# A streaming-encoder step on one core: gathers split in two passes, the last unit and the tail reordered, one decay step one unit later

## What is computed

```python
log_a = log_sigmoid(da @ w_decay + b_decay) / 16          # decays, 4 heads
...
wts = softmax(top_v) * p_g; eid = g_sel * 4 + top_i        # top-1 of 4 groups, top-2 of its 4 experts
y[token] += wts * ((silu(x @ w_gate[e]) * (x @ w_up[e])) @ w_down[e])
x = x + y
y_prompt, y_sample = rms_norm(x, norm_final)
```

## Time and profile before

| | us |
|---|---|
| median of 3 runs | 1055.69 |
| lowest, highest | 1054.32, 1058.29 |
| profiled execution | 1055.09 |
| its span | 1053.3 |
| busy TensorE, VectorE, ScalarE, POOL | 1011.3, 666.0, 539.7, 162.5 |
| granted TensorE clock, mean | 0.989 |

### The profile page before, as it was taken

The page is one execution under the profiler, slowest core; times in us unless marked ns, Lnnn a source line. Parts: engine busy times, 40 slices in busy tenths (PEclk is TensorE's granted clock), DMA queues, the critical chain, the costliest instruction groups (busy, mean ns, idle before and its releaser), DMA issues.

```text
span 1053.3 us, 16974 instructions
## 1 busy us (share of the span) xinstructions
PE 1011.3 (96%) x6950; PEld 899.4 (85%) x6950; DVE 666.0 (63%) x1009; ACT 539.7 (51%) x719; POOL 162.5 (15%) x178
## 2 busy tenths in 40 slices
PE   6999999999999999999999999999999999999984
PEld 4999899998999888888988998787788888888863
DVE  5334753453223366767665666466888989898976
ACT  5236533432223335455575633233588888878853
POOL 2111100000000123332321010031201010101061
PEclk9999999999999999999999999999999999999988
DMA  7877865527355475575363280527999999999765
GB/s 184 201 215 176 164 140 65 96 45 114 58 66 111 106 122 64 81 69 64 101 221 121 70 275 27 214 101 299 413 412 413 413 415 412 415 412 415 315 128 150
DMA packets 126172, 207.55 MB, mean 197 GB/s; under 512 B 11230, under 2 KB 68574, under 8 KB 126099
## 3 DMA queue, kind: packets, MB, share of 16 engines
q1 hardware_dynamic: 110290, 149.38, 52.4%
q0 software_dynamic: 13168, 47.59, 13.2%
q10 hardware_dynamic: 2640, 9.57, 2.3%
HBM read 174.40 MB, written 32.12 MB: 196 GB/s over the span
## 4 chain that ended last, share of the span: by engine, by line
PE 82%; DVE 5%; DMA 5%; ACT 4%; issue 3%; POOL 1%; DVEq 0%; POOLq 0%; ACTq 0%
PE ps L1222 22%; PE ps L1224 22%; PE ps L1223 22%; PE ps L1198 5%; DMA x<-y_rows,rows_i 2%; PE ps L1380 2%; PE ps L1394 2%; DMA x_rows<-h,slot_i 1%; PE ps L1356 1%; ACT w_hi L835 1%; PE ps L1340 1%; PE ps L1495 1%; PE ps L1355 1%; PE ps L1292 1%; DMA xg<-x_rows 1%
## 5 line engine op out<-in xcount | busy, mean ns | idle before, releaser
L1935 DVE TENSOR_TENSOR e_lo<-raw,e_hi 128x2048 fp32r<-128x2048 f32 x96 | 219.3, 2288 | 28.5 <-ACT e_hi L1015 28.4
L1015 ACT ACTIVATE e_hi<-raw 128x2048 fp32r<-128x2048 f32 x96 | 184.0, 1918 | 54.9 <-PE ps L1224 43.9
L1222 PE MATMUL ps<-h_hi,w_hi 128*128 128x272 f32 x632 | 186.7, 295 | 0.0
L1224 PE MATMUL ps<-h_hi,w_lo 128*128 128x272 f32 x632 | 182.3, 288 | 0.0
L1223 PE MATMUL ps<-h_lo,w_hi 128*128 128x272 f32 x632 | 181.9, 288 | 0.0
L1721 DVE TENSOR_TENSOR w_lo<-ring,w_hi 128x2048 fp32r<-128x2048 f32 (+1 forms) x40 | 72.5, 1812 | 80.1 <-ACT w_hi L835 80.1
L835 ACT ACTIVATE w_hi<-ring 128x1024 fp32r<-128x1024 f32 (+1 forms) x56 | 79.6, 1421 | 80.1 <-PE ps L1224 72.6
L1222 PEld LDWEIGHTS ps<-h_hi,w_hi 128*128 128x128 f32 x632 | 119.1, 188 | 1.2 <-issue 0.7
L1223 PEld LDWEIGHTS ps<-h_lo,w_hi 128*128 128x128 f32 x632 | 119.1, 188 | 0.2
L1224 PEld LDWEIGHTS ps<-h_hi,w_lo 128*128 128x128 f32 x632 | 118.8, 188 | 0.0
L1222 PE MATMUL ps<-w_hi,h_hi 128*128 128x256 f32 x384 | 110.0, 287 | 2.6 <-DVE va L2006 2.6
(11 more groups left out here) (432 smaller groups left out, 2040.4 us busy)
## 6 DMA issues: line engine op xcount, KB each, us to landing
raw<-in_w_gate_dram SPq DMA_DIRECT2D x32, 1024.0 KB, 10.8
raw<-in_w_up_dram SPq DMA_DIRECT2D x32, 1024.0 KB, 9.6
raw<-in_w_down_dram SPq DMA_DIRECT2D x32, 1024.0 KB, 9.8
ring<-in_w_in_dram SPq DMA_DIRECT2D x24, 1024.0 KB, 10.6
x_rows<-zero POOLq DMA_DIRECT2D x16, 512.0 KB, 7.6
ring<-in_w_in_dram SPq DMA_DIRECT2D x16, 512.0 KB, 8.4
xg<-x_rows POOLq DMA_DIRECT2D x15, 512.0 KB, 6.2
y_rows<-yo ACTq DMA_DIRECT2D x14, 512.0 KB, 6.5
```

The source lines that it names most:

```text
L1015: act.activation(e_hi[buf][:], raw[slot][:], ACT.Copy).then_inc(s_ehi, 1)
L1222: pe.matmul(out, left[0], right[0], start=first, stop=False)
L1224: return pe.matmul(out, left[1], right[0], start=False, stop=final)
L1935: dve.tensor_tensor(e_lo[slot][:], raw[slot][:], e_hi[buf][:].bitcast(F32), ALU.subtract).then_inc(s_elo, 1)
```

## The change

Seven edits:
1. `dec` 4 is behind va[9] (and behind `dec_apply` 2 there) instead of behind va[8], on all engines.
2. Unit 0: the turned rows of expert 1 come after expert 0's last up part on TensorE; ScalarE and VectorE split one more weight part before them. The row index is made after the gated product and `slot_weights_out`; the overflow counts in unit 1; the one-hots of experts 14 and 15 in units 1 and 2, one each.
3. Row 0 of `y_rows` is the zero row; expert e is stored from row 128 e + 1. The index is made of a lower and a higher slot of each token: the lower one if it is in experts 0 to 12, the other in the second column.
4. POOL: five first gathers (`y_rows[0:EARLY+1]`) once expert 12 is stored, without waiting for one another; then the slot weight of expert 15; after the store of expert 13 the five second ones.
5. Last unit: silu and gated product ahead of one weight part and more, one-hot transposes between expert 15's two down parts.
6. Tail: VectorE adds tile i, then scales tile i-1; ScalarE's square and root follow each add. `overflow` and all the rest for a full expert stand inside the branch, which comes last; in it the outputs would be made and stored a second time.
7. SyncE stores ahead of the branch.

```diff
         for f in range(GH + 2):
-            if f <= GH:
+            if f < GH:
                 hook(units_of["va"][2 * f], "dec", f)
             if f >= 2:
                 hook(units_of["va"][2 * f + 1], "dec_apply", f - 2)
+            if f == GH:
+                hook(units_of["va"][2 * f + 1], "dec", f)
...
@@ sync
+            for i in range(NTILE):
+                store(i, 0)
             with sp.If(n_ovf > 0):
+                sp.wait_ge(s_out[0], 48)
+                sp.wait_ge(s_out[1], 32)
+                sp.wait_ge(s_ovi, 3)
...
@@ gpsimd
             slot_weight(NE - 2)
-            slot_weight(NE - 1)
             pool.wait_ge(s_ovi, 1)
             pool.wait_ge(s_yst[0], 16 * LAST // 2)
+            pool.wait_ge(s_yst[1], 16 * (LAST // 2 - 1))
+            for i in range(NTILE):
+                add_rows(i, 0, rows_i, s_rows[i], y_rows[0:EARLY + 1])
+            slot_weight(NE - 1)
             pool.wait_ge(s_yst[1], 16 * LAST // 2)
-            add_rows(0, 0, rows_i, s_rows[0])
             for i in range(NTILE):
-                if i + 1 < NTILE:
-                    add_rows(i + 1, 0, rows_i, s_rows[i + 1])
                 pool.wait_ge(s_rows[i], 48)
                 add_rows(i, 1, rows_i, s_rows[i])
...
@@ scalar
             part_hi(third_after(0, 1))
+            part_hi(third_after(0, 2))
             x_out(1, 1)
-            for j in range(2, 4):
-                part_hi(third_after(0, j))
+            part_hi(third_after(0, 3))
...
             h_out(r - 1)
-            for j in range(1, 4):
+            for j in range(1, 3):
                 part_hi(third_after(r, j, 1))
             silu(r, part_of(r, 3, 1))
-            part_hi(third_after(r, 4, 1))
+            part_hi(third_after(r, 3, 1))
             act.wait_ge(s_at, NE)
             act.activation(hl_hi[:].rearrange("p c t -> p (c t)"), ps[:, 2], ACT.Copy).then_inc(s_hhi, 1)
+            part_hi(third_after(r, 4, 1))
...
+            act.activation(stat[:, 60:61], eps[:], ACT.Sqrt)
+            for i in range(NTILE):
+                act.wait_ge(s_add, i + 1)
+                squares(i)
             act.wait_ge(s_ovi, 2)
...
@@ tensor
             GU(part_of(0, 2), 0, 2, 6)
+            GU(part_of(0, 3), 0, 3, 6)
             XT(1, 1, 16)
-            GU(part_of(0, 3), 0, 3, 6)
...
             Dn(part_of(r, 5, 1), 5)
-            pe.wait_ge(s_into, 4)
+            pe.wait_ge(s_hlo, NE)
+            last_down(part_of(NE, 4), 4)
+            pe.wait_ge(s_into, 5)
             transposes(P, [(ps[:, (3, 0)[k], P * i:P * i + P], hot[:, k, i]) for k in range(2) for i in range(NTILE - 1)], s_hot)
             transposes(TS, [(ps[:, 1, TS * k:TS * k + TS], hot[0:TS, k, NTILE - 1]) for k in range(2)], s_hot)
-            pe.wait_ge(s_hlo, NE)
-            last_down(part_of(NE, 4), 4)
             last_down(part_of(NE, 5), 5)
...
@@ vector
                 step(dve.tensor_tensor(y_slot, home, ranks, ALU.add))
-                step(dve.tensor_tensor(y_slot, y_slot, away, ALU.add))
-                dve.tensor_scalar(rows_i[:], y_slot, float(LATE), None, ALU.min).then_inc(s_ovi, 1)
+                step(dve.scalar_tensor_tensor(y_slot, y_slot, 1.0, away, ALU.add, ALU.add))
+                low, high = home[:, 0:NTILE], home[:, NTILE:2 * NTILE]
+                step(dve.tensor_tensor(low, y_slot[:, 0:NTILE], y_slot[:, NTILE:2 * NTILE], ALU.min))
...
                 part_lo(third_after(r, 1, odd))
                 if not last:
                     x_out(r + 1, 1 - odd)
+                if isinstance(r, int) and r == 1:
+                    overflow_counts()
                 part_lo(third_after(r, 2, odd))
+                if isinstance(r, int) and r in (1, 2):
+                    last_one_hots(r - 1)
...
             part_lo(third_after(0, 1))
-            rows_index()
-            overflow_counts()
+            part_lo(third_after(0, 2))
             x_out(1, 1)
             gated(0, 0, 6)
             slot_weights_out()
-            for j in range(2, 4):
-                part_lo(third_after(0, j))
+            rows_index()
+            part_lo(third_after(0, 3))
...
-            part_lo(third_after(r, 1, 1))
-            last_one_hots()
-            for j in range(2, 4):
+            for j in range(1, 3):
                 part_lo(third_after(r, j, 1))
             gated(r, 1)
-            part_lo(third_after(r, 4, 1))
+            part_lo(third_after(r, 3, 1))
...
+            add(0)
+            for i in range(1, NTILE):
+                add(i)
+                finish(i - 1, 0)
+            finish(NTILE - 1, 0)
             n_ovf = dve.value_load(ovi[0:1, 0:1], min_val=0, max_val=NOVF)
             with dve.If(n_ovf > 0):
+                dve.wait_ge(s_out[0], 48)
+                dve.wait_ge(s_out[1], 32)
+                overflow()
                 late_rows()
```

More of the change, by code:

```diff
@@ L41 @@
 LATE = LAST * CAP
+EARLY = LATE - CAP
 PARTS, PART, PBUF, RAW = 6, KC * FE // 2, 3, 12
@@ L601, in _ @@
                             load_part(e, j, seq % RAW)
[L602 to L605, removed]
+                for i in range(NTILE):
+                    store(i, 1)
+                sp.wait_ge(s_out[0], 96)
+                sp.wait_ge(s_out[1], 64)
             sp.wait_ge(s_out[0], 48)
@@ L646, in _ @@
             pool.dma_start(S_in[:], state_gla[0, 0].rearrange("h k v -> k h v")).then_inc(s_sin, 16)
-            zero_blocks([(x_rows, ROWS * e) for e in range(NE)] + [(y_rows, LATE + CAP * i) for i in range(NOVF)])
-            pool.dma_start(y_rows[LATE + CAP * NOVF:].rearrange("o (a n) -> (o a) n", n=512), zero[0:2]).then_inc(s_zero, 16)
+            zero_blocks([(x_rows, ROWS * e) for e in range(NE)] + [(y_rows, LATE + 1 + CAP * i) for i in range(NOVF)])
+            pool.dma_start(y_rows[0:1].rearrange("o (a n) -> (o a) n", n=512), zero[0:2]).then_inc(s_zero, 16)
             pool.wait_ge(s_ke_mm, NTILE)
@@ L761, in slot_weight, with add_rows @@
                 pool.tensor_copy(sw_now[:, e % 2:e % 2 + 1], sw[:, e:e + 1]).then_inc(s_swn, 1)
-            def add_rows(i, k, index, done):
+            def add_rows(i, k, index, done, rows=y_rows):
                 n, col = TILES[i][1], k * NTILE + i
-                pool.indirect_dma_start(x2[0:n, i], None, y_rows, bass.IndirectOffsetOnAxis(index[0:n, col:col + 1], 0),
+                pool.indirect_dma_start(x2[0:n, i], None, rows, bass.IndirectOffsetOnAxis(index[0:n, col:col + 1], 0),
                                         compute_op=ALU.add).then_inc(done, 16)
@@ L1101, in y_out @@
                 act.wait_ge(s_y, e + 2 if isinstance(e, int) and e >= NE else e + 1)
-                row = LATE + 1 + (e - NE) * CAP if isinstance(e, int) and e >= NE else e * CAP
+                row = LATE + 1 + (e - NE) * CAP if isinstance(e, int) and e >= NE else e * CAP + 1
                 act.dma_start(y_rows[bass.ds(row, CAP)], yo[:, slot]).then_inc(s_yst[slot], 16)
@@ L1168, in _, with squares @@
             y_kept(NE - 1, 1, 1)
+            def squares(i):
+                n = TILES[i][1]
+                step(act.activation(sqf[0:n], x2[0:n, i], ACT.Square, accum_out=stat[0:n, 50 + i:51 + i]))
+                act.activation(stat[0:n, 55 + i:56 + i], stat[0:n, 50 + i:51 + i], ACT.Sqrt, bias=eps[0:n], scale=1.0 / D).then_inc(s_fsq, 1)
+            act.activation(stat[:, 60:61], eps[:], ACT.Sqrt)
+            for i in range(NTILE):
+                act.wait_ge(s_add, i + 1)
+                squares(i)
             act.wait_ge(s_ovi, 2)
@@ L1186, in _ @@
                 act.wait_ge(s_late, 16 * 2 * NTILE)
[L1187 to L1191, removed]
+                act.wait_ge(s_fo, NTILE)
+                for i in range(NTILE):
+                    squares(i)
         @block.tensor
@@ new lines, in rows_index @@
+                low, high = home[:, 0:NTILE], home[:, NTILE:2 * NTILE]
+                step(dve.tensor_tensor(low, y_slot[:, 0:NTILE], y_slot[:, NTILE:2 * NTILE], ALU.min))
+                step(dve.tensor_tensor(high, y_slot[:, 0:NTILE], y_slot[:, NTILE:2 * NTILE], ALU.max))
+                step(dve.tensor_scalar(away[:, 0:NTILE], low, float(EARLY), float(4 * NE * CAP), ALU.is_le, ALU.mult))
+                step(dve.tensor_tensor(away[:, 0:NTILE], low, away[:, 0:NTILE], ALU.add))
+                step(dve.tensor_tensor(high, high, away[:, 0:NTILE], ALU.min))
@@ new lines, in rows_index, with last_one_hots @@
+                step(dve.scalar_tensor_tensor(rows_i[:, 0:NTILE], low, float(EARLY), low, ALU.is_le, ALU.mult))
+                dve.scalar_tensor_tensor(rows_i[:, NTILE:], high, float(LATE), high, ALU.is_le, ALU.mult).then_inc(s_ovi, 1)
+            def last_one_hots(k):
+                if k == 0:
+                    dve.wait_ge(s_sc[0], 96)
+                    two = [ybase[:, 2 + q].rearrange("p (e i) -> p e i", e=2) for q in range(2)]
+                    dve.wait_ge(s_ovi, 1)
+                    step(dve.tensor_tensor(ybase[:, 1, 0:NTILE], slot_f[:, 0], slot_f[:, 1], ALU.subtract))
```

(6 more changed lines are left out.)

66 lines of the change are left out of this document (30 added, 36 removed).

## The result

| | before | after |
|---|---|---|
| median, us (8 runs each, side by side) | 1055.82 | 1050.68 |
| lowest, highest | 1054.32, 1058.63 | 1049.11, 1052.67 |
| profiled execution, its span | 1055.09, 1053.3 | 1052.25, 1050.5 |

The ratio of after to before is 0.9943, 95% interval 0.9926 to 0.9960: 5.1 us less by the medians, 6.0 by the ratio, 0.5 to 0.6%. The forecast was 1048.1 with 7.6 us of gain. The direction and the range held; by the medians, a third of the forecast gain did not come.

A forecast was written before the change was run, and what follows sets the result against it. TensorE carries 82% of the chain, so time is lost in its waits and at the end. Terms +3.9 - 0.9 - 11.0 + 0.4 = -7.6 took 1055.09 to 1047.5, with the median's 0.6 1048.1; range 1043.5 to 1052.5 us.

The forecast's parts named there:

- Part 1: Last head's decays, one unit later: ScalarE's eviction comes late and TensorE stalls, then runs at low clock; +3.9 us.
- clock term: Behind the stall for the last head's decays: 13 matmuls at granted clock 0.50; +1.25 us, between 0 and 1.3.
- Rival A: Last head's decays: the move costs nothing, as ScalarE's wait ends earlier than queued; 1044.2 us, chance 0.12.
- Part 2: Units 0 to 2 of the experts: 2.6 us gained, 1.7 lost again; net -0.9 us, bounds 0 to -2.6.
- xg wait: Unit 0: TensorE's 2.5 us wait for expert 1's rows is filled by the third up part; gain 2.6 us.
- new wait for hh: Start of unit 2: TensorE waits for the gated product, which VectorE's added small work holds; 1.7 us lost.
- the next weight part is ready ... net -0.9: Units 0 to 2: step-by-step walk of VectorE's queue, from a part ready at 753.2 to the net of -0.9 us.
- Part 3: Last unit and tail: last row 7.6 us sooner, adds and scalings interleaved, value load off the path; -11.0 us in all.
- Rival B: Tail: gathered rows stay last to come, delayed beside weights and expert 13's store; gain 5.5, not 11.0; 1053.6 us, chance 0.14.
- Rival C: Tail gathers run one at a time, the last landing at 1067; some 22 us over before, chance 0.03.
- Rival D: Unit 14: GpSimd's descriptor writing for gathers holds VectorE; +10 us, 1058, chance 0.02.
- The end: After last scaling: VectorE's value load and branch beside the last store, +0.4 us; SyncE's branch, 0 to +0.9, taken as 0.

The follow-up runs named there:

- e1: New kernel with the last head's decays back on their old unit: 1045.98 us, ratio 0.9891 to the kernel before.
- e10: New kernel with the last head's decays back on their old unit and the branch taken early on SyncE and VectorE only: 1043.28 us, ratio 0.9876 to before.
- e11: On top of e10, four small slot steps of the one-hot work on GpSimd in unit 1, both comparisons on VectorE in unit 2: 1042.85 us, ratio 0.9870.
- e2: Kernel before with only the last head's decays put one unit later: 1061.93 us, ratio 1.0050 to before.
- e3: New kernel with the gated product ahead of the overflow counts and one-hots in units 1 and 2: 1050.40 us, ratio 0.9939 to before.
- e4: New kernel with the transposes of expert 1's rows back ahead of expert 0's fourth part, on TensorE alone: 1053.55 us, ratio 0.9963 to before.
- e8: On top of e10, head 3's decays also moved one unit later: 1047.11 us, ratio 0.9908 to before.
- e5: New kernel with the five first-slot gathers started only once expert 13's rows are stored: 1052.50 us, ratio 0.9963 to before.
- e7: New kernel with all five adds ahead of all five scalings on VectorE: 1051.33 us, ratio 0.9952 to before.
- e9: New kernel with the overflow branch taken early on SyncE, ScalarE and VectorE, the tail in both arms: 1050.23 us, ratio 0.9930 to before.

## Why the prediction was right, and where its sizes were off

**Part 1, the decays: forecast +3.9, measured +4.3.** The eight traces with the move have 61.95 on average in the first column (60.47 to 63.19), the four with the code of before 57.69 (before, e1, e10, e11): +4.26; e1 and e2 say 5.5 and 5.3 by their times (e2: 3.7 to 7.0). The mechanism is as written: eviction and restart came within 0.1 us of the forecast. Its clock term was taken as one number, 1.25, and it differs from execution to execution. In e3 the same wait is 2.2 us long and the clock stays at 1.00 behind it; in after it is 3.7 long and the clock behind it is 0.50 for 4.7 us at least. That the sum comes within 0.4 of the mean is in part luck. Rival A (free) is excluded.

**Part 2, units 0 to 2: forecast -0.9, measured -0.7 or +0.8.** The xg wait's 2.6 (e4: 3.0) and the new wait for hh (1.34, forecast 1.7) are there. The traces e10 and e8, with full clock in unit 1, have 55.1 against 55.84: the forecast. Five others of the same code (after, e1, e5, e7, e9) have 56.6 to 56.8, with a low clock 12 to 16 us behind the 4th e_hi. The traces of before and e2 do not have it there. The step that was mis-sized is "the next weight part is ready ... net -0.9": it priced waits alone and gave the clock no term, in a stretch where no row of before showed one. Mean over the seven: 56.23 against 55.80, +0.4.
What TensorE did ahead of that fall (clock 0.5 from 755.4 in after) bears on edit 2:
```profile
750.79 1.03 PE L1221 MATMUL ps<-ident,xg 128*128 128x128 f32 x8
751.66 2.60 PE L1584 MATMUL ps<-ypick,r_hot 128*128 128x16 f32 x20
```
It was never idle, but ran 28 small matmuls in 3.4 us. Edit 2 brought the two groups together; in before a weight part of 12 matmuls stands between them (744.41 to 745.5, and from 748.10). In e4, with the old order back, the clock is 0.96 and 1.00 at that place and low behind the wait for xg instead. So the order is a likely cause, not a shown one: e10, e8 and e11 run the same 28 matmuls and keep clock 1.00, and no run shows what decides between them.

**Part 3: forecast -11.0, measured -11.3.** Products 7.46 (forecast 7.6), adds to last scaling 3.86 (forecast 3.4). Undone part by part: last unit's order 6.73, interleaving 1.06. Rival B is excluded as it was put, since no add waited for rows; e5 brings its condition about and it costs 2.0. The pace of 3.3 us for each gather, from which the cover was worked out, was not that of the issues: in before GpSimd stood idle 1.9 to 2.9 us ahead of four of the ten for the landing of another. Rival C is excluded: the ten issues take 1.4 to 2.9 us each, and except for the wait of 5.78 they follow one another at 0.3 us; the second went out at 1001.54, while the first landed at 1006.65 (the prediction's price for it sums to 21 us over before and not 22, which changes nothing). Rival D is excluded too: VectorE's parts in units 14 and 15 keep 2.29 us beside the gathers. It is GpSimd that is held (last section).

**The end: forecast +0.4, measured +1.4.** SyncE's compare-and-branch is recorded at 1047.19 and its next instruction at 1049.89; VectorE's at 1046.44 and 1049.37, ScalarE's at 1045.76 and 1049.11. So such a branch costs its engine 2.7 to 3.4 us by itself, the value load having ended ahead of it. The trace of before already had this: there VectorE's value load ends at 1040.86, under the last add, its branch is recorded at 1040.89 and its next instruction at 1043.78. The 2.83 us of the earlier trace rows, which the prediction gave to the value load, are the branch. I took SyncE's as 0 because its value was loaded, and that was the mistake. e9, with nothing else changed at the end, gives the 1.36 back. SyncE is the last engine in after; but e9 and e10 moved SyncE's branch and VectorE's together, so what each costs alone is not separated. The Trainium skill (Runtime: NRT & Kernel Launch, Instruction fetch mechanics) says that a taken branch out of the prefetched window waits for a fetch. The lengths agree with it, but no trace here shows the fetch itself; the 0.9 that the prediction set beside the sum for it was due.

Together: +4.3 + 0.4 - 11.3 + 1.4 = -5.2, and the medians differ by 5.1. Of the 2.4 us missing, 1.3 is part 2, 1.0 the end, 0.4 the decays, less 0.3 of part 3. The profiled pair differs by 2.8 only, since the execution after had the low clock in all of the first three columns, and for longer than before in each.

## What to carry to other kernels

Undo each edit of a bundle by itself: the edit of the decays' hook cost 5.5 us of the 11.5 that the others brought. The best kernel that can be told from the rest is e10, the new one without that edit and with the branches of SyncE and VectorE early. Where an engine that feeds the bound is full, moving its work about may only rename the wait (e3); and removing one wait can expose the next that it had hidden (e8). Put a runtime branch into idle time, not behind the last work, and check each engine separately: what was free on VectorE and SyncE held the chain on ScalarE (e9).

## What the runs showed of the hardware

The granted clock falls to 0.5 in some executions and not in others at the same place of the same code. It fell after idle times of 2 to 4 us, and in unit 1 behind 3.4 us of small matmuls without a break (750.79 to 754.20). In the first column of the table such a fall costs 1.2 us (before against e10) to 2.8 (e11 against e10). The new kernel's runs go with it: their mean granted clock is 0.992 in the two fastest (1049.11, 1049.95) and 0.988 in the three slowest (1051.53 to 1052.67).

GpSimd waits for VectorE's weight parts, which read two tiles in SBUF. In e11, GpSimd's and VectorE's timelines:

```profile
753.43 2.17 POOL L789 TENSOR_TENSOR ybase<-slot_f 128x5 f32<-128x5 f32 x1 [1.93 <-DVE rows_i L2173]
755.68 0.22 POOL L790 TENSOR_TENSOR ybase<-onehot,ybase 128x10 f32<-128x10 f32 x1
755.98 2.13 POOL L791 TENSOR_TENSOR ybase<-ybase,slot_f 128x10 f32<-128x10 f32 x1
758.19 0.21 POOL L792 TENSOR_TENSOR ybase<-ybase,iota_r 128x10 f32<-128x10 f32 x1
```
```profile
753.26 2.29 DVE L1972 TENSOR_TENSOR e_lo<-raw,e_hi 128x2048 fp32r<-128x2048 f32 x1
755.74 2.31 DVE L1972 TENSOR_TENSOR e_lo<-raw,e_hi 128x2048 fp32r<-128x2048 f32 x1 [0.18 <-ACT e_hi L1044]
```

A step of 5 or 10 elements takes 0.21 us alone and 2.13 to 2.17 beside a part of VectorE, and ends 0.05 to 0.06 us after it (755.60 and 755.55; 758.11 and 758.05). VectorE's part is 2.29 and 2.31, hardly longer than alone. The Trainium skill (Advanced Engine Details and Errata, the note on the second Vector SBUF port) says that GpSimd instructions and two-port VectorE instructions block each other; the traces agree in one direction, GpSimd waiting. VectorE's parts stay at 2.29 us beside the issue of gathers in after, but the issues are longer beside the parts: of the 130 issues of these gathers in the thirteen traces, the 30 with no such part beside them take 1.35 to 1.57 us, and the 100 others 1.54 to 3.52, 2.42 on average. VectorE's work at that place sets the pace of the gathers.

The store of expert 13's rows, issued at 1009.35 while first gathers were under way, landed at 1017.48, 8.1 us later, and the second gathers waited 5.78 us for it. In e5, where nothing is gathered beside it, it was issued at 1007.51 and landed at 1010.10, 2.6 us later. It is not gathers alone that do this: in after the store of expert 12 took 7.1 us (991.61 to 998.75) beside the weight loads, with the DMA share at 1.01. Early gathers take part of what they give: they delay the very store that the second ones need.
